# Differential attention on one core: the value unit projected within its own head and turned late, and four of ten modulation blocks computed in the last head

## The chip, the cores and the metric

The kernel runs on one core of one Trainium2 chip. The metric is the device time of one execution in microseconds (us), median of several runs. Engines: PE (TensorE) multiplies matrices, ACT (ScalarE), DVE (VectorE) and POOL (GpSimd) work elementwise, SP (SyncE) issues most of the transfers (DMA). Each engine works through its own instructions in program order and waits at semaphores, so one late operand holds up everything behind it on that engine.

## The reference

One step of a two-layer backbone: attention and a gated feed-forward layer (FFN), then an mLSTM layer and a second FFN. The change lies in the first layer's modulation and attention. `c` and `c_ctx` give the modulation of latent and context tokens:

```python
cond_p = jax.nn.silu(c_ctx)
cond_s = jax.nn.silu(c)
...
    mod_p = jnp.split(cond_p @ ada_w[i] + ada_b[i], 6, axis=-1)
    mod_s = jnp.split((cond_s @ ada_w[i] + ada_b[i])[:, None, :], 6, axis=-1)
    hp = modulate(xp, mod_p[0], mod_p[1])
    hs = modulate(xs, mod_s[0], mod_s[1])
...
        qs, ks_, vs = da_project(hs, da_w_qkv[j])
        k_all = jnp.concatenate([cache_k[:, j], rope_2d(ks_)], axis=1)
        v_all = jnp.concatenate([cache_v[:, j], vs], axis=1)
        ys = da_output(diff_attend(rope_2d(qs), k_all, v_all, lam), da_subln[j], lam_init, da_w_o[j])
...
    xs = post_norm(xs, mod_s[2] * ys, ln_g[i, 0], ln_b[i, 0])
    hs = modulate(xs, mod_s[3], mod_s[4])
```

Here the model width is 1024, there are 128 context and 512 latent tokens (640 in all), 8 heads with two 64-wide maps each and values 128 wide, and 128 cached keys and values. `diff_attend` is softmax of map 0 minus lambda times softmax of map 1, times the values. `mod[0]`, `mod[1]` are needed before the first projection; `mod[2]` first after the output projection, `mod[3]` to `mod[5]` later still.

## The kernel before

**Layout.** Activations lie with features on the partitions: 8 blocks of 128 features by 640 tokens. Everything is 32-bit; a product keeps its accuracy by splitting both operands into a high and a low part: ACT makes the high part (`whi`, `Hh`), POOL or DVE the rest (`wlo`, `Hl`), and PE multiplies high by high, low by high and high by low.

**Units.** A projection unit is 128 output columns: `q`, `k` or `v` of one head, 512 KB of weights. It is 8 tiles of 6 products each (three terms by two halves of the tokens), summed in the PSUM buffer `pj`; ACT copies it out (`evac`, L1216) before the next unit may start in the same buffer. Units run in the order q0 k0 v0 q1 k1 v1 and so on. SP loads unit n once the weights of unit n-2 are split; ACT splits (L1211), then POOL (L481).

**A head.** `head(h)` on PE mixes two things, in an order written out by hand: the attention of head h, and tiles of later units to fill PE's waits. Attention has five stages `st` (one of context tokens, four of latent ones). In a stage PE computes the scores (L811), DVE their maximum (L2039, `nmax`), ACT the exponentials (L1393), DVE the difference of the two maps (L2049 to L2054, `combine`), PE turns that by transposes into `psT` (L827, `turn`), and ACT and DVE copy it out in two parts (L1404, L2065, `turned`). `psT` is one buffer: each turn waits for `t_free` of the one before. `turn_v` (L862) turns the head's values, also in `psT`; ACT and DVE copy them out (L1443 and L1444 `values_hi`, L2095 and L2096 `values_lo`). `values_ctx` (L837) and `values_lat` (L846) multiply by the values; `values_lat` of a head runs in the next one. `rms` (L854) sums squares for the head's norm. A head takes 24 tiles of later units, except the last two: head 6 has 17, head 7 has none and takes six tiles of the output projection (`wo`).

**Rotation.** q and k are rotated (`rotate`, L2071 to L2075) with a swapped copy `sx`, which eight small transfers make (`swap`, L407, queued on SP). `sx` is one buffer: the swap of k0 waits until q0 is rotated.

**Modulation.** A block is 512 columns of `w_ada`, in 4 units of 512 KB (two feature blocks each). `block` (L660) multiplies the condition vectors by them, as rows of a PSUM tile; `copy_rows` (L1785) copies the rows to SBUF, `ada_turn` (L673) turns them, `add_bias` (L1776) adds the bias. Before, the prologue does 10 blocks: 4 ahead of everything and 6 among the projection of units 2 and 3, from an 11-deep ring of buffers `awr`. The other 14 are done in the FFN from a ring of four, `fwr`. The first latent stage of head 0 waits for `mods_ready`, which the second `add_bias` gives.

Of the kernel before, what the change touches and what calls it, by code (L numbers as in the profile page):

```python
# [157 lines left out]
def hybrid_step(nc, a, o):  # L158

    ctx = ExitStack()  # L160
    with ctx:
# [31 lines left out]
        rs = sb("rs", [P, 2, HALF])  # L193
        h32t = sb("h32t", [P, 2, TP])
        h32 = [h32t[:, k, :] for k in range(2)]
        pick = sb("pick", [P, 2 * RUN])


        with ExitStack() as s:
# [12 lines left out]
            condf = sb("condf", [P, KT, PAD + 32], F32, s)  # L212
        with ExitStack() as s:
# [4 lines left out]
            conda = sb("conda", [P, KT, PAD + 32], F32, s)  # L218
        with ExitStack() as s:
            O32 = sb("O32", [P, KT, TP], F32, s)  # L220
            v32 = sb("v32", [P, TP], F32, s)
            Qh = [sb(f"Qh{k}", [P, TP], F32R, s) for k in range(2)]
            Ql = [sb(f"Ql{k}", [P, TP], F32R, s) for k in range(2)]
            KW = TP + PAST
            Kh = [sb(f"Kh{k}", [P, KW], F32R, s) for k in range(2)]
            Kl = [sb(f"Kl{k}", [P, KW], F32R, s) for k in range(2)]
# [7 lines left out]
            rope = sb("rope", [P, 2, LAT], F32, s)  # L234
            ckv = sb("ckv", [P, 2, P], F32, s)
# [44 lines left out]
        pj = [ps(f"pj{k}", [P, 2, 512]) for k in range(1)]  # L280
        with ExitStack() as s:
# [34 lines left out]
        mods_ready = sem("mods_ready")  # L316
        mur_ready, side_ready = sem("mur_ready"), sem("side_ready")
# [45 lines left out]
        def _(sp):  # L363
# [23 lines left out]
            def load_qkv(v):  # L387
                load(a["w_qkv"][v], v // 2, v % 2, D, first=v < 2)
# [28 lines left out]
            load_ada(range(16, 27))  # L417
            sp.dma_start(rope[:, :, :], a["rope"]).then_inc(rope_in, 16)
            swap(0, 0)
            load_ada(range(27, 35))  # L420
            swap(0, 1)
            load_ada(range(35, 39))
            load_qkv(4)
            load_ada(range(39, 4 * NB))
            load_qkv(5)
            for v in range(6, U_WO + 2):
                load(a["w_qkv"][v] if v < U_WO else a["w_wo"][v - U_WO], v // 2, v % 2, D)
                if v % 3 < 2:
                    swap(v // 3 - 1, v % 3)
# [182 lines left out]
        def _(pe):  # L612
# [253 lines left out]
            def head(h):  # L866
# [10 lines left out]
                if nxt:  # L877
                    qkv(q, [7])
# [1634 lines left out]
```

## Time and profile before

| | |
|---|---|
| time, median of 3 runs | 1831.74 us (1829.88 to 1832.03) |
| the profiled execution, its own time | 1830.12 us |
| its span | 1828.3 us |
| PE busy over the span | 95% |
| DVE, ACT, POOL busy | 59%, 39%, 35% |
| prologue, up to the first scores of head 0 | 84.3 us |
| from one head's first scores to the next, heads 2 to 5 | 37.55 to 37.58 us |
| head 6; head 7 up to its `rms` | 36.07 us; 45.28 us |

Times are us from the span's start. In a timeline a row is start, length, engine, line, operation, output<-inputs, and in brackets how long the engine had been idle and what ended that. In a table of stretches a row is the stretch, its length, then busy time with the number of instructions for PE, PE's weight loads, DVE, ACT and POOL, then the granted PE clock as a share of 2.4 GHz, the busy share of the DMA engines and GB/s.

### The profile page before, as it was taken

To read this page: it belongs to the slowest core of one execution; us is meant where nothing else is said; L and a number is where in the kernel's file an instruction comes from. 1 tells how busy PE (TensorE), PEld (TensorE's weight loads), DVE (VectorE), ACT (ScalarE), POOL (GpSimd) and SP (SyncE) were. 2 spreads that over 40 slices of the span, in tenths; PEclk is the share of its full clock that TensorE was granted. 3 is DMA by queue.
4 is the path that set the end of the run, shared out by engine and by line. 5 is a ranking of instruction groups with operands and counts; after the bars stand their busy time and mean duration, and the time that the engine had idled before them with its cause. 6 is when DMAs were issued, how large, how long until landed. Compare 5 with 4: busy or idle time off the path is not lost.

```text
span 1828.3 us, 30131 instructions
## 1 busy us (share of the span) xinstructions
PE 1728.4 (95%) x11412; PEld 1608.8 (88%) x11412; DVE 1070.4 (59%) x1745; ACT 711.2 (39%) x1153; POOL 644.4 (35%) x319
## 2 busy tenths in 40 slices
PE   6899999789999999999998999998889999999996
PEld 3688888678889999999997999997879999999996
DVE  1277776657755614666457545544678781377735
ACT  3255555535432212223246544644363331132324
POOL 3312121236533333333454222222655333233343
PEclk8999999889999999999999999999999999999998
DMA  9722122111355223453211111110212222222221
GB/s 376 266 71 69 54 67 69 34 33 61 116 195 201 82 75 115 151 207 125 80 55 53 47 58 59 47 53 24 70 47 74 75 83 78 69 70 75 87 80 58
DMA packets 55191, 169.42 MB, mean 93 GB/s; under 512 B 7856, under 2 KB 15408, under 8 KB 55088
## 3 DMA queue, kind: packets, MB, share of 16 engines
q1 hardware_dynamic: 48752, 163.79, 26.1%
q10 hardware_dynamic: 6336, 4.20, 0.7%
q8 instruction: 72, 1.18, 0.3%
q14 instruction: 31, 0.25, 0.0%
HBM read 159.04 MB, written 4.72 MB: 90 GB/s over the span
## 4 chain that ended last, share of the span: by engine, by line
PE 70%; DVE 8%; POOL 7%; issue 5%; ACT 5%; DVEq 3%; DMA 2%; ACTq 1%; SPq 0%; POOLq 0%
PE pj L635 58%; POOL wlo L519 4%; DMA awr<-in_w_ada 2%; PE mO L1065 2%; PE psO L846 2%; PE psS L811 1%; PE pfrow L660 1%; POOL ss L533 1%; PE psT L827 1%; DVE pr L2054 1%; ACT pr L1393 1%; ACTq L1266 1%; POOL X L572 1%; DVE sm L2039 1%; PE mS L1021 1%
## 5 line engine op out<-in xcount | busy, mean ns | idle before, releaser
L481 POOL TENSOR_TENSOR wlo<-wraw,whi 128x1024 fp32r<-128x1024 f32 (+1 forms) x124 | 320.5, 2585 | 814.0 <-ACT whi L1211 814.0
L635 PE MATMUL pj<-Hh,whi 128*128 128x320 f32 x2368 | 568.6, 319 | 22.5 <-ACT Hh L1756 4.2
L635 PE MATMUL pj<-Hl,whi 128*128 128x320 f32 x2368 | 548.9, 311 | 3.0 <-POOL Hl L504 2.0
L635 PE MATMUL pj<-Hh,wlo 128*128 128x320 f32 x2368 | 550.7, 311 | 0.0
L635 PEld LDWEIGHTS pj<-Hh,whi 128*128 128x128 f32 x2368 | 397.8, 190 | 53.6 <-issue 37.0
L635 PEld LDWEIGHTS pj<-Hl,whi 128*128 128x128 f32 x2368 | 401.2, 190 | 4.6 <-POOL Hl L504 3.1
L635 PEld LDWEIGHTS pj<-Hh,wlo 128*128 128x128 f32 x2368 | 402.3, 190 | 0.3
L1211 ACT CAST whi<-wraw 128x1024 fp32r<-128x1024 f32 (+1 forms) x175 | 194.2, 1110 | 281.5 <-PE pj L635 241.2
L1959 DVE SCALAR_TENSOR_TENSOR fcv<-fus,vec,fcv 128x127 f32<-128x127 f32 (+1 forms) x176 | 229.1, 1343 | 15.1 <-issue 15.1
L1837 DVE SCALAR_TENSOR_TENSOR X<-pj,mods,X 128x128 f32<-128x128 f32 (+5 forms) x120 | 45.4, 434 | 219.5 <-PE pj L635 219.3
L635 PE MATMUL pj<-Gh,whi 128*128 128x320 f32 x704 | 168.8, 311 | 0.8 <-POOL wlo L519 0.8
L635 PE MATMUL pj<-Gh,wlo 128*128 128x320 f32 x704 | 167.5, 309 | 0.0
L635 PE MATMUL pj<-Gl,whi 128*128 128x320 f32 x704 | 167.5, 309 | 0.0
L1216 ACT COPY fus<-pj 128x640 f32<-128x640 f32 x88 | 60.7, 692 | 212.9 <-PE pj L635 212.7
L1962 DVE SCALAR_TENSOR_TENSOR fcv<-fus,vec,fcv 128x127 f32<-128x127 f32 (+1 forms) x176 | 120.2, 724 | 15.1 <-issue 15.1
L1956 DVE TENSOR_SCALAR fcv<-fus,vec 128x640 f32<-128x640 f32 x88 | 58.8, 668 | 107.5 <-ACT fus L1216 107.5
L635 PEld LDWEIGHTS pj<-Gh,whi 128*128 128x128 f32 x704 | 119.5, 188 | 1.6 <-POOL wlo L519 1.3
L519 POOL TENSOR_TENSOR wlo<-wraw,whi 128x1408 fp32r<-128x1408 f32 (+2 forms) x28 | 83.6, 2985 | 104.2 <-ACT whi L1211 101.9
L635 PEld LDWEIGHTS pj<-Gh,wlo 128*128 128x128 f32 x704 | 119.5, 188 | 0.3
L635 PEld LDWEIGHTS pj<-Gl,whi 128*128 128x128 f32 x704 | 119.5, 188 | 0.0
L1351 ACT CAST Gh<-fpr 128x640 f32 (+1 forms) x44 | 32.0, 728 | 214.3 <-DVE fpr L1981 214.3
L564 POOL TENSOR_TENSOR wlo<-wraw,whi 128x1024 fp32r<-128x1024 f32 x25 | 61.8, 2473 | 133.2 <-ACT whi L1211 133.2
(311 smaller groups left out, 2173.0 us busy)
## 6 DMA issues: line engine op xcount, KB each, us to landing
wraw<-in_w_up SPq DMA_DIRECT2D x88, 512.0 KB, 3.5
fwr<-in_w_ada SPq DMA_DIRECT2D x56, 512.0 KB, 5.9
wraw<-in_w_dn SPq DMA_DIRECT2D x32, 704.0 KB, 4.1
awr<-in_w_ada SPq DMA_DIRECT2D x40, 512.0 KB, 10.9
wraw<-in_w_qkv SPq DMA_DIRECT2D x24, 512.0 KB, 3.5
wraw<-in_w_mlin SPq DMA_DIRECT2D x24, 512.0 KB, 3.4
sx<-h32t SPq DMA_DIRECT2D x128, 32.0 KB, 2.0
wraw<-in_w_wo SPq DMA_DIRECT2D x8, 512.0 KB, 3.5
```

Of the source, the lines that this page charges most:

```text
L481: nc.gpsimd.tensor_tensor(wlo[k][:, 0:width], wraw[k][:, 0:width], whi[k][:, 0:width].bitcast(F32), ALU.subtract).then_inc(w_lo, 1)
L519: nc.gpsimd.tensor_tensor(wlo[k][:, c0:width], wraw[k][:, c0:width], whi[k][:, c0:width].bitcast(F32), ALU.subtract).then_inc(w_lo, 1)
L564: nc.gpsimd.tensor_tensor(wlo[v % 2][:, 0:width], wraw[v % 2][:, 0:width], whi[v % 2][:, 0:width].bitcast(F32), ALU.subtract).then_inc(w_l ...
L635: last = mm(out[:, c, 0:HALF], w, x[:, j, c * HALF:(c + 1) * HALF], start=(j == 0 and n == 0), stop=(j == n_k - 1 and n == 2))
L846: last = mm(psO[:, :], v_[par][:, c, :], t_[:, c, :], start=(c == 0 and n == 0), stop=(c == 4 and n == 2))
L1065: last = mm(mO[:, w, 0:P if part == 0 else 2 * P], v_, t_, start=(c == 0 and n == 0), stop=(c == len(terms) - 1 and n == 2))
L1211: nc.scalar.copy(whi[k][:, 0:width], wraw[k][:, 0:width]).then_inc(w_hi, 1)
L1216: nc.scalar.copy(dst.rearrange("p (a b) -> p a b", a=2), pj[k if pairs == 2 else 0][:, :, 0:HALF]).then_inc(pj_copied, 1)
L1837: last = stt(out=x, in0=pj[k][:, bank, c0:c1], scalar=gt, in1=x, op0=ALU.mult, op1=ALU.add)
L1956: ts(c[:, :], f[:, :], tap[1], bias, ALU.mult, ALU.add)
L1959: stt(out=c[:, t0 + 1:t1], in0=f[:, t0:t1 - 1], scalar=tap[0], in1=c[:, t0 + 1:t1], op0=ALU.mult, op1=ALU.add)
L1962: last = stt(out=c[:, t0:t1 - 1], in0=f[:, t0 + 1:t1], scalar=tap[2], in1=c[:, t0:t1 - 1], op0=ALU.mult, op1=ALU.add)
```

## The change

Four edits that belong together.

- **Units in another order.** `QKV_ORDER`: q0 k0 q1 k1 v0 q2 k2 v1 ... q7 k7 v6 v7. The value unit of head h is projected within head h, where v of head h+1 was.
- **Turned late.** `turn_v(h)` and `values_ctx(h)` move to the end of head h (in heads 0 to 6), on ACT and DVE too; `rms(h-1)` stands between them.
- **One unit less ahead, one more behind.** The prologue projects units 0 and 1 and seven tiles of unit 2; head 6 now has 24 tiles, and head 7 the last tile of v7.
- **Six blocks in the prologue, four in the last head.** Their 16 units are loaded into four buffers that lie over `rope`, the q and k buffers of even heads and `h32t`; they are summed in `pj` (`lrow`), so no tile of `wo` starts before `lmods_ready`. The six tiles of `wo` of head 7 follow after `scores(h, 4)`.

The unit v0 is turned with the others; `cond` is padded once, not twice. The diff, cut to its core:

```diff
+NP = 6
...
-        order += [("v", h), ("t", 5 * h), ("t", 5 * h + 1), ("t", 5 * h + 2), ("t", 5 * h + 3)]
+        if h == DA_HEADS - 1:
+            order.append(("v", h))
+        order += [("t", 5 * h), ("t", 5 * h + 1), ("t", 5 * h + 2), ("t", 5 * h + 3)]
+        if h < DA_HEADS - 1:
+            order.append(("v", h))
...
+    if what == "q":
+        return 3 * h - 1 if h else 0
+    if what == "k":
+        return 3 * h if h else 1
+    return min(3 * h + 4, 3 * DA_HEADS - 1)
...
+            def load_last():
+
+                for u in range(4 * (NB - NP)):
+                    if u == 0:
+                        sp.wait_ge(roped, 2 * DA_HEADS)
+                    elif u < 3:
+                        sp.wait_ge(sc_done, 5 * (DA_HEADS - 1))
+                    elif u == 3:
+                        sp.wait_ge(qk_ready, 2 * DA_HEADS)
+                        sp.wait_ge(kv_out[0], 16 * DA_HEADS)
+                    else:
+                        sp.wait_ge(lw_used, u - 3)
+                    sp.dma_start(lwr[u % 4][:, :, :].rearrange("p a n -> p (a n)"), a["w_ada"][4 * NP + u]).then_inc(lw_landed[u % 4], 16)
...
-            load_ada(range(16, 27))
+            load_ada(range(16, 4 * NP))
             sp.dma_start(rope[:, :, :], a["rope"]).then_inc(rope_in, 16)
             swap(0, 0)
-            load_ada(range(27, 35))
             swap(0, 1)
-            load_ada(range(35, 39))
             load_qkv(4)
-            load_ada(range(39, 4 * NB))
             load_qkv(5)
+            swap(1, 0)
...
+                scores(h, 0)
+                qkv(q, [7])
+                if prev:
+                    turn(h - 1, 4)
+                qkv(k, [0, 1])
+                if prev:
+                    values_lat(h - 1)
+                scores(h, 1)
+                qkv(k, [2, 3, 4])
+                turn(h, 0)
+                qkv(k, [5, 6])
+                scores(h, 2)
+                qkv(k, [7])
+                turn(h, 1)
+                qkv(v, [0, 1, 2, 3])
+                scores(h, 3)
+                qkv(v, [4])
+                turn(h, 2)
+                qkv(v, [5, 6, 7])
+                scores(h, 4)
+                qkv(q2, [0])
+                turn(h, 3)
+                qkv(q2, [1, 2, 3])
+                turn_v(h)
+                qkv(q2, [4, 5])
+                if prev:
+                    rms(h - 1)
+                qkv(q2, [6])
+                values_ctx(h)
+
+            def last_head(h):
...
                 scores(h, 0)
+                qkv(3 * DA_HEADS - 1, [7])
+                turn(h - 1, 4)
+                last_blocks([0, 1])
+                values_lat(h - 1)
                 scores(h, 1)
                 turn_v(h)
+                last_blocks([2, 3])
                 turn(h, 0)
+                last_blocks([4])
                 scores(h, 2)
+                last_blocks([5])
                 turn(h, 1)
                 values_ctx(h)
+                last_blocks([6, 7])
                 scores(h, 3)
                 turn(h, 2)
+                last_turn()
                 scores(h, 4)
+                pe.wait_ge(lmods_ready, 1)
+                wo([0])
                 turn(h, 3)
+                wo([1, 2, 3])
+                rms(h - 1)
+                wo([4, 5]).then_inc(part_used, 1)
...
             first_pair(0, h_ready, 0, 0)
             ada_block(4)
+            qkv(2, [0, 1])
             ada_block(5)
-            qkv(2, [0, 1, 2, 3])
-            ada_block(6)
...
-            qkv(3, [6])
+            qkv(2, [2, 3, 4, 5, 6])
             ada_turn(1)
...
+            def last_head(h):
+                combine(h - 1, 4)
+                nmax(h, 0)
...
+                combine(h, 2)
+                nmax(h, 3)
+                copy_last()
+                turned(h, 2)
+                combine(h, 3)
+                nmax(h, 4)
+                dve.wait_ge(lrow_turned, 1)
+                add_bias(lmod, 4 * NP, NB - NP)
+                turned(h, 3)
```

**SP's queue at the end of the prologue.** SP before, from the last loads ahead of `rope`; `awr` are modulation units, `sx` the swaps of q0 and then k0.

```order
L377 DMA awr<-in_w_ada 128x1024 x11
L418 DMA rope<-in_rope 128x1024
L407 DMA sx<-h32t 16x512 x8
L377 DMA awr<-in_w_ada 128x1024 x8
L407 DMA sx<-h32t 16x512 x8
L377 DMA awr<-in_w_ada 128x1024 x4
L371 DMA wraw<-in_w_qkv 128x1024
L377 DMA awr<-in_w_ada 128x1024
L371 DMA wraw<-in_w_qkv 128x1024 x2
L407 DMA sx<-h32t 16x512 x8
```

SP in the changed kernel, from the same place.

```order
L404 DMA awr<-in_w_ada 128x1024 x8
L459 DMA rope<-in_rope 128x1024
L448 DMA sx<-h32t 16x512 x16
L398 DMA wraw<-in_w_qkv 128x1024 x2
L448 DMA sx<-h32t 16x512 x8
L398 DMA wraw<-in_w_qkv 128x1024
L448 DMA sx<-h32t 16x512 x8
```

The two swaps now stand next to each other (x16): 13 modulation loads between and behind them are gone, and three of the eleven ahead of `rope`.

**PE's queue at the end of head 2.** PE before, from `rms` to the next head's first scores.

```order
L635 MATMUL pj<-Hl,whi 128x320 x2
L854 MATMUL psT<-ss,ones 128x320 x2
L635 MATMUL pj<-Hh,whi 128x320 x2
L635 MATMUL pj<-Hh,wlo 128x320 x2
L635 MATMUL pj<-Hl,whi 128x320 x2
L635 MATMUL pj<-Hh,whi 128x320 x2
L635 MATMUL pj<-Hh,wlo 128x320 x2
L635 MATMUL pj<-Hl,whi 128x320 x2
L635 MATMUL pj<-Hh,whi 128x320 x2
L635 MATMUL pj<-Hh,wlo 128x320 x2
L635 MATMUL pj<-Hl,whi 128x320 x2
L811 MATMUL psS<-Kh,Qh 128x128
```

PE in the changed kernel, from `turn_v` (L919) over `rms` (L911) to the first product of `values_ctx` (L894), behind whose three products the next head's scores stand.

```order
L919 MATMUL psT<-ident,v 128x128 x5
L680 MATMUL pj<-Hh,whi 128x320 x2
L680 MATMUL pj<-Hh,wlo 128x320 x2
L680 MATMUL pj<-Hl,whi 128x320 x2
L680 MATMUL pj<-Hh,whi 128x320 x2
L680 MATMUL pj<-Hh,wlo 128x320 x2
L680 MATMUL pj<-Hl,whi 128x320 x2
L911 MATMUL psT<-ss,ones 128x320 x2
L680 MATMUL pj<-Hh,whi 128x320 x2
L680 MATMUL pj<-Hh,wlo 128x320 x2
L680 MATMUL pj<-Hl,whi 128x320 x2
L894 MATMUL psO<-Aph,Vh 128x128
```

`turn_v` and `values_ctx` now stand here; they stood behind the scores and behind the turn of stage 1. `rms` has one tile and `values_ctx` behind it where it had three tiles.

**PE's queue in the middle of head 7.** PE before: the turn of stage 1, `values_ctx`, two tiles of `wo`, the scores of stage 3.

```order
L827 MATMUL psT<-ident,pr 128x128 x5
L837 MATMUL psO<-Aph,Vh 128x128
L837 MATMUL psO<-Apl,Vh 128x128
L837 MATMUL psO<-Aph,Vl 128x128
L635 MATMUL pj<-Hh,whi 128x320 x2
L635 MATMUL pj<-Hh,wlo 128x320 x2
L635 MATMUL pj<-Hl,whi 128x320 x2
L635 MATMUL pj<-Hh,whi 128x320 x2
L635 MATMUL pj<-Hh,wlo 128x320 x2
L635 MATMUL pj<-Hl,whi 128x320 x2
L811 MATMUL psS<-Kh,Qh 128x128
```

PE in the changed kernel: between `values_ctx` and the scores stand the four units of the fourth block.

```order
L705 MATMUL pj<-lwk,condp 32x512 x2
L705 MATMUL pj<-lwh,condp 32x512 x2
L884 MATMUL psT<-ident,pr 128x128 x5
L894 MATMUL psO<-Aph,Vh 128x128
L894 MATMUL psO<-Apl,Vh 128x128
L894 MATMUL psO<-Aph,Vl 128x128
L705 MATMUL pj<-rope,condp 32x512 x2
L705 MATMUL pj<-lwq,condp 32x512 x2
L705 MATMUL pj<-lwk,condp 32x512 x2
L705 MATMUL pj<-lwh,condp 32x512 x2
L868 MATMUL psS<-Kh,Qh 128x128
```

The scores of stage 3 now stand behind products that wait for transfers.

## Rows read from the trace of the kernel before

**Rows 1.** Busy time by stretch: end of prologue, head 4, head 6, head 7.

```profile
52.00:84.20 32.20, 28.30 (x195) 16.99 (x194) 7.11 (x11) 6.63 (x10) 7.08 (x3) 1.00 0.75 275
230.24:267.80 37.56, 36.36 (x247) 32.54 (x247) 27.29 (x49) 20.50 (x42) 7.21 (x3) 1.00 0.22 64
305.35:341.42 36.07, 31.36 (x205) 26.80 (x204) 25.82 (x48) 19.05 (x40) 6.09 (x3) 0.95 0.23 67
341.42:386.70 45.28, 35.27 (x189) 28.96 (x189) 25.58 (x43) 21.68 (x44) 12.74 (x8) 0.81 0.04 12
```

**Rows 2.** Chain that ended last, in the prologue: start, us, what.

```profile
63.37 3.73 PE pj L635 x24
...
70.98 10.35 DMA awr<-in_w_ada
...
84.28 0.49 PE psS L811 x6
```

**Rows 3.** Timeline of SP in the prologue, the two swaps.

```profile
52.49 5.01 SPq L407 DMA_DIRECT2D sx<-h32t  x8
...
62.56 4.93 SPq L407 DMA_DIRECT2D sx<-h32t  x8
```

**Rows 4.** Timeline of DVE in the prologue: rotations, k0's low part, rows copied.

```profile
59.00 0.98 DVE L2071 TENSOR_TENSOR sx<-sx,rope 128x512 f32<-128x512 f32 x1 [8.53 <-DMA sx<-h32t]
...
60.66 0.69 DVE L2075 TENSOR_TENSOR h32t<-h32t,sx 128x512 f32<-128x512 f32 x1
...
74.27 0.69 DVE L2071 TENSOR_TENSOR sx<-sx,rope 128x512 f32<-128x512 f32 x1 [11.30 <-DMA sx<-h32t]
...
77.13 0.83 DVE L2088 TENSOR_TENSOR Kl<-h32t,Kh 128x640 fp32r<-128x640 f32 x1 [0.21 <-ACT Kh L1438]
82.47 0.69 DVE L1785 COPY arow<-prow 128x512 f32<-128x512 f32 x1 [4.51 <-PE prow L660]
```

**Rows 5.** Timeline of PE in head 4: `turn_v`, two turns, first of `values_ctx`.

```profile
239.51 0.76 PE L862 MATMUL psT<-ident,v 128*128 128x128 f32 x5
...
247.59 0.77 PE L827 MATMUL psT<-ident,pr 128*128 128x128 f32 x5 [0.37 <-DVE pr L2054]
248.11 0.31 PE L837 MATMUL psO<-Aph,Vh 128*128 128x128 f32 x1
...
260.72 0.77 PE L827 MATMUL psT<-ident,pr 128*128 128x128 f32 x5 [0.45 <-DVE pr L2054]
```

**Rows 6.** Timeline of ACT in head 4: values copied out, high part.

```profile
240.31 0.58 ACT L1443 CAST Vh<-psT 128x512 fp32r<-128x512 f32 x1 [1.47 <-PE psT L862]
```

**Rows 7.** Timeline of DVE in head 4: last low values; `combine` at head's end.

```profile
241.86 0.28 DVE L2096 TENSOR_TENSOR Vl<-psT,Vh 128x128 fp32r<-128x128 f32 x1
...
265.06 2.39 DVE L2051 TENSOR_TENSOR sm<-sm,lam 128x1 f32<-128x1 f32 x1
```

**Rows 8.** Timeline of POOL in head 4, the third unit's low part.

```profile
265.01 2.42 POOL L481 TENSOR_TENSOR wlo<-wraw,whi 128x1024 fp32r<-128x1024 f32 x1 [9.94 <-ACT whi L1211]
```

**Rows 9.** Busy time by stretch in heads 6 and 7, where the clock was low.

```profile
339.00:351.60 12.60, 9.30 (x26) 6.51 (x27) 7.65 (x15) 5.13 (x12) 5.51 (x3) 0.50 0.13 42
368.70:375.30 6.60, 5.34 (x25) 4.51 (x25) 4.63 (x9) 2.66 (x6) 0.43 (x1) 0.50 0.00 0
```

**Rows 10.** Timeline of PE in head 7: scores of stages 2 and 3, last turn.

```profile
358.96 0.33 PE L811 MATMUL psS<-Kh,Qh 64*128 64x128 f32 x1
...
364.57 0.32 PE L811 MATMUL psS<-Kh,Qh 64*128 64x128 f32 x1 [0.57 <-ACT pr L1393]
...
379.04 0.77 PE L827 MATMUL psT<-ident,pr 128*128 128x128 f32 x5 [0.28 <-DVE pr L2054]
```

**Rows 11.** Timeline of DVE in head 7: `combine` of stage 2, last step.

```profile
365.49 2.23 DVE L2054 SCALAR_TENSOR_TENSOR pr<-pr,sm 128x640 f32<-128x640 f32 x1
```

**Rows 12.** Timeline of PE in the FFN: one modulation block.

```profile
496.24 1.92 PE L660 MATMUL pfrow<-fwr,condf 128*32 128x512 f32 x16
```

**Rows 13.** All instructions on the tile `fwr`: issue to landing, units of 512 KB.

```profile
DMA to landing us min/median/max: 3.5/5.9/7.8
```

More of the change, by code:

```diff
@@ L111, with _qkv_unit @@
 QT = (4, 0, 1, 2, 3)
+def _qkv_unit(what, h):
+    if what == "q":
[3 more added lines that the diff above has]
+    return min(3 * h + 4, 3 * DA_HEADS - 1)
+QKV_ORDER = [at for _, at in sorted((_qkv_unit(what, h), 3 * h + c) for h in range(DA_HEADS) for c, what in enumerate("qkv"))]
 GROWS = 100
@@ L316, in hybrid_step @@
         mods_ready = sem("mods_ready")
+        lw_landed = [sem(f"lw_landed{k}") for k in range(4)]
+        lw_used, lrow_copied, lrow_turned, lmods_ready = (
+            sem(n) for n in ("lw_used", "lrow_copied", "lrow_turned", "lmods_ready"))
         mur_ready, side_ready = sem("mur_ready"), sem("side_ready")
@@ L651, in first_pair, with block @@
                         tile(pair, k, [j], pairs=2, terms=(2,))
-            def block(b, n, out, conds, bufs, landed, used, at):
-                for kp in range(4):
+            def block(b, n, out, conds, bufs, landed, used, at, kps=range(4)):
+                for kp in kps:
                     u = at + kp
@@ L866, in head @@
             def head(h):
-                nxt, nxt2, prev, last = h + 1 < DA_HEADS, h + 2 < DA_HEADS, h > 0, h + 1 == DA_HEADS
-                q, k, v, q2 = (3 * h + 3 + c for c in range(4))
+                prev = h > 0
+                q, k, v, q2 = (3 * h + 2 + c for c in range(4))
+                scores(h, 0)
[28 more added lines that the diff above has]
+            def last_head(h):
                 def wo(ks):
@@ L1466, in head @@
             def head(h):
-                nxt, prev, last = h + 1 < DA_HEADS, h > 0, h + 1 == DA_HEADS
-                k, v, q2, k2 = (3 * h + 4 + c for c in range(4))
-                if nxt:
-                    copy_q(h + 1)
+                prev = h > 0
+                copy_q(h + 1)
                 if prev:
@@ L1778, in add_bias @@
                     last.then_inc(mods_ready, 1)
+                if t0 == 4 * NP:
+                    last.then_inc(lmods_ready, 1)
                 dve.drain()
             def copy_rows(k):
-                dve.wait_ge(aw_used, 4 * NB if k else 16)
+                dve.wait_ge(aw_used, 4 * NP if k else 16)
                 if k:
@@ L2140, in _ @@
             dve.wait_ge(row_turned, 2)
-            add_bias(pmod[1], 2 * KT, 6)
-            for h in range(DA_HEADS):
+            add_bias(pmod[1], 2 * KT, NP - 4)
+            for h in range(DA_HEADS - 1):
                 head(h)
+            last_head(DA_HEADS - 1)
             combine(DA_HEADS - 1, 4)
```

205 lines of the change are left out of this document (99 added, 106 removed).

## The prediction

> **What bounds the kernel now.** I read four stretches, each by its table of busy time, then its timelines, and the chain for the prologue. In the end of the prologue the DMA engines are busy for 0.75 of the time and PE gets through 28.3 us of short work in 32.2 [rows 1]; the chain there runs through a modulation load that takes 10.35 us to come, and reaches head 0's first scores at 84.28 [rows 2]. A middle head is PE's: 36.36 us busy of 37.56 [rows 1]. What is left are three short waits, two of them for DVE's difference of the maps, 0.37 and 0.45 us [rows 5]. Head 6 has 17 tiles and is hardly shorter, 36.07 us. Head 7 is 45.28 us with a mean clock of 0.81 [rows 1]: there the serial chain of a stage (scores, maximum, exponentials) sets the pace, 5.6 us from one stage's scores to the next [rows 10], and the clock is at half for 12.6 and 6.6 us [rows 9]. So the change has a load-bound stretch to shorten, seven full stretches in which every added PE instruction counts, and one with room in it whose order matters.
>
> The sum is made on the profiled execution, 1830.12 us with a span of 1828.3; it is 1.6 us under the median of the three runs, 1831.74.
>
> **1. Prologue: -11.0.** Head 0's scores need k0 rotated. Its swap is issued at 62.56 [rows 3] and lands only at 74.27, for which DVE waited 11.30 us [rows 4]: eight modulation loads were queued ahead of it. Without them the swap may be issued when q0 is rotated, 60.66 + 0.69 = 61.35 [rows 4]. q0's own swap was issued at 52.49 [rows 3] and DVE started at 59.00 [rows 4], 6.5 us later; so k0 starts at 67.85. From there to k0's low part is 77.13 + 0.83 - 74.27 = 3.7 us, and from the copy of the rows to the scores 84.28 - 82.47 = 1.8 us [rows 2, 4], since that copy stands behind k0 on DVE: 73.35. Before it was 84.28. PE is through by about 65: two blocks and seven tiles (0.93 each, 3.73 for four [rows 2]) from 52. The four removed blocks cost nothing else here. Bounds: -12 if the swap also issues faster, -9 if the two loads of units 4 and 5 get in its way.
>
> **2. Clock at the restart: +1.5.** PE is now idle for some 8 us before head 0. In head 6 the clock fell to 0.50 after waits of 2 to 3 us and stayed there 12.6 us, and later 6.6 [rows 9]. Low for 3 to 6 us of mostly PE-bound work costs half of that, less the waits in it: 1.5, between 0 and 3. The gap itself is in no row before; if the clock stayed up, the sum would be 1.5 less.
>
> **3. The late turn: +6.0.** Per head, from the order on PE:
> - `turn_v` leaves the place behind the scores of stage 1. Its five transposes last 0.76 [rows 5] with their drain, under which the next product starts; I take 0.5. That gives nothing: the turn of stage 1 waits for DVE [rows 5], and DVE's chain starts at those scores (maximum, exponentials, rotation of q, difference), none of which gets shorter. The wait grows from 0.37 to 0.9 us.
> - `values_ctx` leaves, about 0.4 (three products, the first [rows 5]): -0.4, and all behind it moves up, the next wait for DVE too, as its chain starts at the scores of stage 3.
> - At the end `turn_v` comes back, +0.6 with the change of operand type, and `values_ctx`, +0.4.
> - `rms` needs `psT`, which `values_lo` now frees. ACT starts 0.8 us after `turn_v` (239.51 to 240.31 [rows 5, 6]); its two copies take 0.75 (0.58 the first [rows 6]), DVE's two subtractions 0.9 (0.28 the last [rows 7]), with the hand-overs 2.6 us. PE covers 0.5 + 2 x 0.93 = 2.35 of it: +0.25.
>
> Together 0.6 + 0.25 = 0.86 us a head; seven heads, less the first, which has no `rms`: 6.0. At a head's end DVE also runs into POOL: an operation on 128x1 took 2.39 us, from 265.06, beside POOL's 2.42 from 265.01 [rows 7, 8]. It does so in both kernels; `combine` of the last stage then comes 0.9 later, just as the head does. Bounds: 0.5 (no wait at `rms`) and 1.3 a head (0.4 more where ACT is late with the values), so 3.5 to 9. The other moved edits of ACT and DVE sit in their idle time (20.5 and 27.3 us busy of 37.56 [rows 1]) and cost nothing; if `values_hi` met the exponentials it would cost their 1.6 us, which is in the upper bound.
>
> **4. Head 6 gets its seven tiles back: +1.5.** It lasted 36.07, full ones 37.56 [rows 1].
>
> **5. Head 7: +5.2.** It begins at full clock now. Times from its first scores, work at full clock:
> - A last tile of v7 (0.9), its copy, the block of four units that landed in head 6 (1.9 [rows 12]), then `values_lat`: scores of stage 1 at 7.9 (before 11.4, at half clock).
> - The ring is four buffers. A unit's buffer is free when PE has used it, and the next one lands 3.5 us after issue alone, up to 7.8 as the fourth of four [rows 13], so 1.3 to 1.4 apart. Units 4 to 7 are used at 10.3 to 11.7; unit 9, issued at 10.8, lands at 15.2. Scores of stage 2 stand behind it: 15.75. The chain alone would have let them go at 14.1.
> - Unit 15 is issued at 18.2 and lands at 22.4; the scores of stage 3 stand behind it: 23.0 (before 23.15 [rows 10], so still even). Then one free chain: scores of stage 4 at 27.85.
> - `wo` must wait for `lmods_ready`. On DVE that stands behind `combine` of stage 3 and the maximum of stage 4. `combine` will meet POOL's low part of `wo`'s input, as it did once before in this head, 2.23 us for one step instead of 0.9 [rows 11]. It ends at 31.1, the maximum at 33.0, the bias at 33.3. PE idles for 4 us.
> - Then six tiles of `wo` (5.4), a turn, `rms`, one tile more: last turn at 41.1. Before it was at 379.04 - 341.42 = 37.6 [rows 1, 10]. So +3.5, and what follows is the same.
> - The idle 4 us bring the clock down again: +1.7 (low 3 to 5 us, half lost [rows 9]).
>
> The Trainium skill (SBUF — State Buffer, Who interferes with whom) says that of a DVE operation with two SBUF inputs and a GpSimd operation that reads SBUF the later one is blocked until the other is through, and that copies and scalar operations between SBUF tiles can be caught too. By it the small operation behind the maximum of stage 4 could be caught as well, for as long as the step in [rows 11] was, 1.3 us more.
>
> Bounds for head 7: +1 (units land 3.5 us apart from issue each, no POOL collision, no low clock) and +10 (all transfers like the slowest in [rows 13], and the clock low through the second half).
>
> **Sum.** -11.0 + 1.5 + 6.0 + 1.5 + 5.2 = +3.2: 1833.3 us for an execution like the profiled one, 1834.9 on the median. I give 1834.5. The padding of the condition vectors that goes from the FFN (one copy and one memset on DVE) was under DVE's slack: nothing, at most -0.7.
>
> **Rivals.**
> - **A. Faster, about 1824.** `turn_v` late costs nothing, because PE's waits for DVE shrink as much as the end of the head grows, and head 7's blocks fall into its waits (10 us idle of 45.28 [rows 1]): -11.0 + 1.5 + 1.5 + 0 to 1 = -7.5. For it: PE waits three times in a head. Against it: the waits hang on a chain that starts at PE's own scores. It decides where the head period stays at 37.6.
> - **B. Slower, about 1840.** Head 7's tail: everything that waited for `pj` comes after the scores of stage 4. If the bias is ready only after the whole stage (ACT's exponentials of stage 4 ahead of DVE), and the clock stays at half through the six tiles of `wo` (5.4 us more), the head costs 10 to 11 instead of 5.2: +8 to +9. It decides if the idle time before `wo` is over 5 us. For it: the half clock after shorter gaps [rows 9]. Against it: the chain of DVE as written ends at 33.3.
> - **C. The prologue does not shorten as said**, since something else than the loads holds k0 (the copy of v0, which also leaves, or unit 3's split): gain 5 instead of 11, +9, about 1840. Against it: the 11.30 us wait names the swap's DMA [rows 4].
>
> **How the numbers follow.** Chances: forecast 0.52, A 0.15, B 0.28, C 0.05. A change of 0.2% is 3.7 us, about what a measurement of this kernel can tell from none. The forecast's own range, 1827 to 1837, crosses that limit on both sides: of its 0.52 some 0.07 is slower and 0.03 faster. So faster 0.15 + 0.03 = 0.18, same 0.42, slower 0.28 + 0.05 + 0.07 = 0.40. The range, 1826 to 1842, leaves out most of A and the far ends of B and C.
>
> **What the changed profile would show.** Step 1: first scores of head 0 at 73 to 75, DVE's wait for the swap under 7 us. Step 2: half clock at the start of head 0. Step 3: heads 38.2 to 38.7 us apart, a short wait of `rms` for the low values. Step 4: head 6 as long as the others. Step 5: head 7 some 48 to 52 us, with waits of the last blocks of modulation for `w_ada` and one of 4 us before the first tile of `wo`. What would make me wrong: a head period under 38, or a tail of head 7 in which `wo` is not held.

## The result, and the profile after

The changed kernel takes 1839.18 us (median of five runs, 1837.65 to 1841.11), the kernel before 1829.95 beside it (five runs): ratio 1.0050, 95% interval 1.0039 to 1.0062. It is slower by 0.5%, some 9 us. The profiled executions differ by 7.5 us (1837.65 against 1830.12). The value forecast was 1834.5 and the range 1826 to 1842; slower had a chance of 0.40, no measurable change 0.42.

I read four stretches of the changed kernel. Busy time by stretch: end of the prologue, head 4, head 6, head 7 up to its `rms`, and the part of head 7 at half clock (columns as in [rows 1]):

```profile
62.00:73.20 11.20, 6.13 (x38) 5.86 (x36) 4.09 (x8) 0.72 (x1) 0.00 (x0) 0.87 0.36 115
225.06:263.28 38.22, 36.54 (x247) 32.58 (x247) 27.29 (x49) 20.38 (x43) 7.23 (x3) 1.00 0.21 63
301.55:339.78 38.23, 36.53 (x247) 32.57 (x247) 27.28 (x49) 20.39 (x43) 7.22 (x3) 1.00 0.38 118
339.78:394.23 54.45, 46.36 (x268) 32.10 (x267) 25.82 (x44) 22.50 (x46) 14.51 (x8) 0.91 0.38 137
371.00:381.30 10.30, 8.38 (x39) 7.81 (x39) 5.61 (x9) 3.33 (x8) 3.62 (x2) 0.52 0.00 0
```

Beside [rows 1]: head 4 is 0.66 us longer for 0.18 us more PE work, head 6 is now a full head, and head 7, up to its `rms`, has grown from 45.28 to 54.45.

The prologue, on DVE (k0's swap, its low part, the copy of the rows) and then on PE:

```profile
67.08 0.69 DVE L2144 TENSOR_TENSOR sx<-sx,rope 128x512 f32<-128x512 f32 x1 [4.90 <-DMA sx<-h32t]
...
69.93 0.83 DVE L2161 TENSOR_TENSOR Kl<-h32t,Kh 128x640 fp32r<-128x640 f32 x1 [0.20 <-ACT Kh L1498]
70.67 0.68 DVE L1855 COPY arow<-prow 128x512 f32<-128x512 f32 x1
```

```profile
71.41 1.87 PE L732 MATMUL pmod<-pick,arow 128*128 128x4 f32 x8 [5.07 <-DVE arow L1855]
73.20 0.48 PE L868 MATMUL psS<-Kh,Qh 64*128 64x128 f32 x2
```

The swap's wait fell from 11.30 [rows 4] to 4.90 us and the first scores came at 73.20 for 84.22. But PE stood idle for 5.07 us first, and then the turn of the rows took 1.87 us, at half clock.

A middle head, on PE (turn of stage 1, turn of the values, `rms`, first of `values_ctx`):

```profile
242.29 0.77 PE L884 MATMUL psT<-ident,pr 128*128 128x128 f32 x5 [0.76 <-DVE pr L2127]
...
258.32 0.71 PE L919 MATMUL psT<-ident,v 128*128 128x128 f32 x5
260.88 1.31 PE L911 MATMUL psT<-ss,ones 128*128 128x320 f32 x4
262.90 0.22 PE L894 MATMUL psO<-Aph,Vh 128*128 128x128 f32 x1
```

The turn of stage 1 waits 0.76 us where it waited 0.37 [rows 5]: taking the values' turn away from before it only lengthened the wait.

Head 7, the chain of work that ended last (start, us, what). The two transfers in it are loads of `w_ada`; the last four lines are `wo`'s first tile and what it waited for (DVE's maximum of stage 4, the small operation behind it, and the drain behind the bias):

```profile
351.39 4.76 DMA lwq<-in_w_ada
...
357.25 1.36 PE psS L868 x10
...
360.00 5.78 DMA lwh<-in_w_ada
...
366.88 1.37 PE psS L868 x10
...
370.65 1.87 PE pj L724 x8
372.53 2.40 PE psS L868 x10
...
374.96 1.49 DVE sm L2112
...
376.52 0.17 DVE sm L2114
...
376.69 0.10 DVEq L1849
...
376.84 1.97 PE pj L680 x6
```

The scores of stages 2 and 3 stand behind loads. PE's waits in this head, two for loads of `w_ada` and the two in the tail, ahead of the turn of the row and of `wo`:

```profile
354.94 1.05 PE L705 MATMUL pj<-rope,condp 128*32 128x512 f32 x4 [1.94 <-DMA rope<-in_w_ada]
...
364.56 1.05 PE L705 MATMUL pj<-lwk,condp 128*32 128x512 f32 x4 [1.42 <-DMA lwk<-in_w_ada]
...
370.65 1.87 PE L724 MATMUL pj<-pick,v 128*128 128x8 f32 x8 [1.72 <-DVE v L1860]
...
376.84 0.90 PE L680 MATMUL pj<-Hh,whi 128*128 128x320 f32 x2 [1.92 <-DVE mods L1844]
```

From the turn of the row (L724) to about 381 all of PE's work is at half clock (1.2 of 2.4 GHz): the scores of stage 4 take 2.40 us for 1.37.

Where the 7.5 us lie, in us, from the first scores of each head in the two traces: first scores -11.0; head 0 +3.2; head 1 +1.3; heads 2 to 5 +2.8; head 6 +2.2; head 7 up to its `values_lat` +9.1 (49.16 for 40.03).

### The profile page after: what moved, and what is told of

It is laid out like the page before. It is cut to its first block, busy times and chain, and to the rows that moved or that the text cites. A ratio compares the mean times of both kernels' runs of the same rounds, so it can differ in the third digit from the quotient of the medians.

```text
span 1835.9 us, 30150 instructions
## 1 busy us (share of the span) xinstructions
PE 1732.7 (94%) x11420; PEld 1613.8 (88%) x11420; DVE 1070.0 (58%) x1745; ACT 710.6 (39%) x1153; POOL 644.5 (35%) x319
## 4 chain that ended last, share of the span: by engine, by line
PE 71%; DVE 8%; POOL 6%; issue 5%; ACT 4%; DVEq 2%; DMA 2%; ACTq 1%; SPq 1%; POOLq 0%
PE pj L680 59%; POOL wlo L564 4%; PE mO L1124 2%; PE psS L868 2%; PE psO L903 2%; PE pfrow L705 1%; DMA awr<-in_w_ada 1%; POOL ss L578 1%; PE psT L884 1%; ACTq L1325 1%; DVE pr L2127 1%; DVE sm L2112 1%; PE mS L1080 1%; DVE h32t L2148 1%; ACT pr L1452 1%
```

## The experiments

Each is compared with the kernel before on the same chip. The runs fall into three sets on three chips (e1 to e4, e5 to e8, e9 to e12), in which the kernel before had medians of 1829.96, 1829.50 and 1830.00 us. Times are medians; the lengths are from one profiled execution each, so a difference of lengths and one of medians need not agree. Heads 0 and 4 are counted from their first scores to those of the next head, head 7 from its first scores to its `values_lat`.

| run | us | ratio to before (95%) | first scores | head 0 | head 4 | head 7 |
|---|---|---|---|---|---|---|
| before | 1829.50 to 1830.00 | | 84.22 | 33.02 | 37.56 | 40.03 |
| changed | 1839.18 | 1.0050 (1.0039 to 1.0062) | 73.20 | 36.18 | 38.22 | 49.16 |
| e1, turn only | 1836.53 | 1.0037 (1.0024 to 1.0049) | 83.59 | 35.95 | 38.21 | 36.78 |
| e2, blocks only | 1832.43 | 1.0021 (1.0011 to 1.0032) | 74.98 | 33.56 | 37.58 | 51.67 |
| e3, four loads | 1832.39 | 1.0012 (1.0003 to 1.0021) | 72.98 | 36.27 | 38.27 | 43.08 |
| e4, filler | 1836.32 | 1.0030 (1.0017 to 1.0043) | 73.06 | 34.91 | 38.25 | 49.34 |
| e5, early hand-over | 1832.91 | 1.0019 (1.0009 to 1.0028) | 73.84 | 36.04 | 38.22 | 42.67 |
| e6, e2 with ring of 8 | 1829.06 | 0.9996 (0.9987 to 1.0005) | 76.04 | 34.54 | 37.58 | 46.13 |
| e7, e6 and e5's edit | 1822.40 | 0.9966 (0.9955 to 0.9976) | 75.85 | 34.56 | 37.56 | 41.55 |
| e8, changed with ring of 8 | 1831.93 | 1.0017 (1.0008 to 1.0026) | 73.50 | 36.06 | 38.25 | 42.82 |
| e9, e7, a block in head 6 | 1826.05 | 0.9980 (0.9972 to 0.9989) | 74.76 | 33.37 | 37.55 | 43.59 |
| e10, e8 and e5's edit | 1826.99 | 0.9984 (0.9975 to 0.9993) | 72.19 | 35.96 | 38.26 | 38.77 |
| e11, before, turn twice | 1833.54 | 1.0023 (1.0015 to 1.0032) | 84.10 | 33.56 | 38.09 | 40.35 |
| e12, changed, turn twice | 1845.90 | 1.0089 (1.0075 to 1.0104) | 71.83 | 36.50 | 38.79 | 51.31 |

**The two halves of the change: e1 and e2.** e1 is the changed kernel with all blocks in the prologue (their loads placed as before) and none in head 7:

```
-NP = 6
+NP = 10
...
             turn(h, 0)
-            last_blocks([4])
+            wo([0, 1])
             scores(h, 2)
...
-            last_turn()
+            wo([4])
             scores(h, 4)
-            pe.wait_ge(lmods_ready, 1)
```

> The changed kernel with all ten modulation blocks back in the prologue (loads and products interleaved as before), no block and no turn of them in head 7, and wo's six tiles back in their old places there. What is left of the change is the unit order with the late turn of the values. Theory T (the head period read from the changed trace): 38.25 us for 37.55 in heads 0 to 5 (+4.2), head 6 full for 36.07 (+2.2), one more tile in head 7 (+0.9), nothing in the prologue: +7.3 us, 1837. Rival R (the order of the units costs little, and nearly all of the loss is the blocks in head 7): +1 to +3, 1831 to 1833.

e2 is the other half, the blocks moved with the units in their old order (an edit of the changed kernel):

```
-    return min(3 * h + 4, 3 * DA_HEADS - 1)
+    return 3 * h + "qkv".index(what)
...
                 scores(h, 1)
+                turn_v(h)
...
                 turn(h, 1)
+                values_ctx(h)
...
-                turn_v(h)
...
-                values_ctx(h)
```

> The other half: unit order, early turn of the values and weights' queue as before, but blocks 6 to 9 in head 7 with their loads, turn and bias as in the changed kernel. Theory T: prologue -11.0, head 0 +3.7 (clock at half and the wait for the first copy), head 7 +8 (9.2 less the tile of the value unit): +0.7 us, 1830.7, between 1828 and 1833. If the turn and the blocks are independent, this and the run of the turn alone add up to the changed kernel (+9.2 by the medians). Rival R (the blocks are the loss): 1836 to 1838.

The turn and order alone cost 6.6 us, the blocks alone 2.5; together 9.0, the change 9.2 (by the ratios 0.37% and 0.21% for 0.50%). Both totals are what theory T said, and the rival (most of the loss is the blocks) falls. The parts behind the totals are not what T said, so that they agree is in part luck:

- e1: head 0 grew by 2.9 us, where T had 0.7, and head 7 became 3.3 us shorter, where T had 0.9 more. Before, head 7 runs at a mean clock of 0.79; in e1, whose head 6 has tiles to its end, at 0.91.
- e2: the first scores came 9.2 us earlier (T: 11.0), head 0 grew by 0.5 (T: 3.7), head 7 by 11.6 (T: 8). The blocks alone thus pay 11.6 us in head 7 for 9.2 in the prologue.

In e1's trace head 4 is as long as in the changed kernel, and its head 0 is long too, though its first scores are as late as before; I had put that down to the shorter prologue. Head 0 of e1, of e2, and the first tile of its second unit in e1 and in e2:

```profile
83.59:119.54 35.95, 33.81 (x224) 30.82 (x223) 23.38 (x45) 16.89 (x36) 5.86 (x3) 0.91 0.18 52
```

```profile
74.98:108.54 33.56, 31.26 (x224) 28.45 (x223) 23.99 (x45) 17.16 (x37) 6.44 (x3) 1.00 0.22 65
```

```profile
86.91 0.87 PE L682 MATMUL pj<-Hh,whi 128*128 128x320 f32 x2 [0.93 <-ACT h32t L1278]
```

```profile
77.54 0.53 PE L669 MATMUL pj<-Hh,whi 128*128 128x320 f32 x2 [0.93 <-ACT h32t L1275]
```

The wait of 0.93 us is the same in both kernels (and before), but the clock is at half in e1, from 84.2 on, and at full in e2. What differs ahead of the fall, between e1 and the kernel before, are the eight tiles of unit v0, which the kernel before and e2 have in the prologue and the late order has not. In e2 PE's tiles go on up to 74.1, just ahead of the first scores; in e1 PE stands idle six times between 70 and 83, 4.35 us in all, for loads and for the copy of the rows. The late turn, which e1 has too, is not what brings the clock down, since it stands behind the fall; but no run puts the eight tiles back alone. Nor are they the whole story: e6, e7 and e9 have e2's prologue and head 0, and in e6 and e7 the clock fell in head 0 too, for 3.4 us, and it took 34.5 to 34.6 us. With the tiles head 0 took 33.0 to 34.6 us, without them and without the filler of e4 36.0 to 36.3 (six kernels).

**The clock at the restart: e4.** 32 products in PE's gap, whose results nothing reads:

```
             qkv(2, [2, 3, 4, 5, 6])
+            for _ in range(32):
+                mm(psS[:, 0:HALF], whi[0][:, 0:P], Hh[:, 0, 0:HALF], start=True, stop=True)
             ada_turn(1)
```

> The changed kernel with 32 products of 128x320 put into the 5.07 us in which PE waits for the copy of the rows in the prologue; they write the scores' bank, which head 0's scores overwrite, so no result hangs on them. Theory T (the fall of the clock to 0.50 is what head 0 lost: turn of the rows 1.87 us at half clock, tiles at 0.73 for 0.46 a pair up to 80.9): 3 to 4 us less, 1835.5. Rival (head 0's chain is what counts and the low clock hides behind it, or the clock falls nevertheless): 0 to -1, 1838 to 1839.

1836.32 us, 2.9 less by the medians; in the profiled execution head 0 is 1.27 us shorter. The median is near theory T, the trace between the two: the clock stayed up through the turn and the first tile, and then was at half behind the wait of 0.93 us nevertheless. Busy time of e4 in steps of 2 us:

```profile
74.00:76.00 2.00, 1.07 (x7) 0.84 (x6) 0.27 (x2) 1.22 (x5) 0.00 (x0) 0.96 0.01 4
76.00:78.00 2.00, 2.00 (x10) 2.00 (x9) 0.87 (x4) 1.12 (x3) 0.81 (x1) 0.50 0.17 38
```

The changed kernel, e3, e5, e8 and e10 have one prologue and one head 0, and head 0 took 35.96 to 36.27 us in them; e4's 34.91 lies 1.0 to 1.4 us below all five. So much of the 3.2 us in head 0 is shown to be the low clock; the filler doesn't remove all of it, and how much the rest of it costs was not measured.

**The loads of head 7: e3, e8, e6.** e3 issues only four of the sixteen, so it leaves out the weights of blocks 7 to 9:

```
-                for u in range(4 * (NB - NP)):
+                for u in range(4):
```

> The changed kernel with only the first four of the sixteen loads of w_ada in head 7: blocks 7, 8 and 9 take the weights of block 6, so the modulation they give is that of block 6's weights. All products, the turn, the bias and the order stay. Theory T (the ring of four buffers delays the scores of stages 1 to 3: waits of 1.94, 1.42 and some 0.8 us in head 7, and they bring the clock down): head 7 shorter by 4 to 7 us, 1832 to 1835. Rival (the serial chain of a stage sets the pace, and a wait for a load only takes the place of one for the chain): -1 or less, 1838 to 1839.

Head 7 is 43.08 for 49.16, the time 6.8 us less: theory T, but for one part of it. That the waits for loads bring the clock down is not borne out: without them head 7 has a mean clock of 0.88, with them 0.90. The cause could still be the depth of the ring or the bandwidth. e8 and e6 keep all loads and lay four more buffers over tiles 4 to 7 of `Hh` and `Hl`, which nothing reads after the last value tile:

```
-            lwr = [rope, lwq, lwk, lwh]
+            lwr = [rope, lwq, lwk, lwh, lwx[0][1], lwx[1][1], lwx[0][0], lwx[1][0]]
...
-                        sp.wait_ge(lw_used, u - 3)
+                        sp.wait_ge(lw_used, u - 7)
```

> The changed kernel itself with the ring of eight; here the four new buffers are free only when the last value tile is done early in head 7, so they stand behind the four old ones in the ring. Theory T: units 4 to 7 are issued some 8 us earlier than now, the waits of 1.94, 1.42 and 0.8 us go: -3 to -5 us, 1835. Rival (bandwidth): -1 or less, 1838.5.

> The kernel with only the blocks moved (before's unit order), its ring of w_ada units made eight deep: four more buffers lie in the tiles 4 to 7 of Hh and Hl, free once the last value unit's product is done in head 6, and they come first in the ring, so half of the sixteen units are under way before head 7. Same work and order otherwise. Theory T (head 7 waits for loads because only four can be under way; run with four loads: 6 us): 4 to 6 us less than the kernel with only the blocks moved, 1826.5 to 1828.5. Rival (DMA bandwidth, not the depth, is the bound): -1 or less, 1831.5.

Head 7 of e8:

```profile
339.90:382.72 42.82, 37.05 (x240) 25.29 (x240) 26.75 (x44) 21.17 (x44) 13.02 (x8) 0.92 0.46 174
```

That is no longer than with twelve loads left out, and the time is 7.3 us less than the changed kernel's, more than T's 3 to 5 (6.0 by the ratios). Depth was the bound, bandwidth was not. e8's waits for loads in head 7 are down to two of 0.23 us. In e6, with before's order, head 7 is 5.5 us shorter than in e2, as T said, but the medians differ by only 3.4 (4.6 by the ratios); in e6's profiled execution head 0 was 1.0 us longer than e2's, though nothing was changed there.

**The hand-over and the held `wo`: e5.** The row is copied earlier and turned into `psO`; in place of `wo`, `values_lat` at the end of the head waits for `lmods_ready`, and the bias stands on DVE ahead of `combine` of stage 3. The edit, cut:

```
-        lmod = pj[0][:, 1, 0:32].rearrange("p (q w) -> p q w", q=4)
+            lmod = psO[:, 0:32].rearrange("p (q w) -> p q w", q=4)
...
+                if h == DA_HEADS - 1:
+                    pe.wait_ge(lmods_ready, 1)
...
                 last_turn()
+                wo([0, 1])
                 scores(h, 4)
-                pe.wait_ge(lmods_ready, 1)
-                wo([0])
+                wo([2])
                 turn(h, 3)
-                wo([1, 2, 3])
+                wo([3])
...
                 combine(h, 2)
+                copy_last()
                 nmax(h, 3)
-                copy_last()
                 turned(h, 2)
+                dve.wait_ge(lrow_turned, 1)
+                add_bias(lmod, 4 * NP, NB - NP)
                 combine(h, 3)
...
```

> The changed kernel with the hand-over of head 7's blocks made earlier and wo not held by it: DVE copies the row ahead of the maximum of stage 3 instead of behind it, the turn of the row goes to the bank of psO, which is free then, so wo's tiles in pj wait only for the copy; two tiles of wo before the scores of stage 4, one before the turn of stage 3, one behind it, two behind rms. Same work. Theory T (the tail of head 7 pays for being held: waits of 1.72 and 1.92 us, and with them the clock at half for 10 us): last turn 46.8 to about 42 us behind the head's start, -4 to -5 us, 1834.5. Rival (the chain of stages 3 and 4 sets the end, the held wo only fills it): -0 to -1.5, 1838.

Head 7 with the edit:

```profile
340.19:382.86 42.67, 37.40 (x240) 23.79 (x239) 25.78 (x44) 21.29 (x44) 13.09 (x8) 1.00 0.49 175
```

Head 7 is 6.5 us shorter in the profiled execution, and the medians differ by 6.3, more than T's 4 to 5. The clock fits that: 1.00 for the whole of head 7, where it was 0.90. The two waits (1.72 and 1.92 us) were 3.6 us; with them went the stretch at half clock. How the 6.5 us divide between the two was not measured. The turn of the row had to leave `pj` altogether, since a tile of `wo` writes both halves of `pj`. The Trainium skill (PSUM — Partial Sum Buffer, Summary: rules for kernel authors) says that PSUM read while a matmul runs should be in a different bank than the one written, and `psO` is one. No run here shows what a shared bank would do.

**Both repairs, in before's order and in the late one: e7, e10.**

> Blocks moved, before's unit order, ring of eight, and the early hand-over with wo not held. Theory T (load waits and held wo are two separate costs): about 1823, 7 us under before. Rival (only one of them is on the path at a time): as the better of the two, 1827.

> The changed kernel with both repairs of head 7 (ring of eight, early hand-over of the row with wo not held) and its late turn of the values kept. Theory T (late turn and unit order cost 6.6 us by themselves, whatever head 7 does): 1822.4 + 6.5, so 1828 to 1829, no better than before. Rival (the early turn's gain overlaps with the repairs): 1824 to 1825.

e7 takes 1822.40 us, 0.34% under the kernel before, about what T said; it is the fastest version. In before's order the ring gave 3.4 us and the hand-over 6.7 on top of it (medians). Whether the two costs are separate is seen in the changed kernel's order, where all four versions were run: head 7 is 49.16 us as it was, 42.82 with the ring (e8), 42.67 with the hand-over (e5), 38.77 with both (e10). The gains are 6.3, 6.5 and 10.4: separate for the most part, and 2.4 us are counted in both.

e10 is 4.6 us slower than e7 by the medians (0.18% by the ratios), less than the 6.5 expected and more than the rival's 2 to 3. The profiled executions don't show that difference: they are 0.3 us apart, 1826.86 for e10, which is near its median, and 1826.52 for e7, which is the second longest of its eleven (1820.24 to 1827.18). In them e10 is 7.6 us longer from first scores to head 7 (266.4 for 258.8), which is the late turn, the full head 6 and the clock of head 0; its first scores are 3.7 earlier and its head 7 is 2.8 shorter. It has full clock in head 7, where e7 has half up to 341 and again from 362 to 365. The granted clock over the whole of e7's execution was 0.978 in the profiled one and 0.981 to 0.983 in the six shortest, which suggests that these had less half clock; no trace shows where. Head 7 of e7 and of e10:

```profile
334.64:376.19 41.55, 37.00 (x234) 24.92 (x233) 27.86 (x45) 20.36 (x42) 11.73 (x8) 0.88 0.44 164
```

```profile
338.58:377.35 38.77, 35.86 (x241) 23.71 (x240) 26.52 (x44) 21.27 (x44) 13.10 (x8) 1.00 0.50 192
```

**What a turn of the values costs in each place: e11, e12.** Five transposes done twice, in the kernel before and in the changed one:

```
-                for c in range(5):
+                for c in (0, 1, 2, 3, 4, 0, 1, 2, 3, 4):
```

> The kernel before with the five transposes of the values done twice in their early place, the second five over the first: 0.46 us more PE work a head. Theory T of the late turn (behind the scores of stage 1 the turn lies under the wait for DVE's difference of the maps, 0.37 us, and on the path only with the rest): the wait goes to nothing and the head period grows by about 0.1 us, 37.55 to 37.65, in all +1 us, not more than the measurement can tell. Rival (PE's work counts wherever it stands): +0.46 a head, 38.0, in all +3.5 us.

> The changed kernel with the same doubling in the late place. Theory T: nothing there waits for DVE's maps, so all of it is paid, +0.45 us a head, 38.25 to 38.7, +3 us in all. Rival (the wait of rms for the values' low part takes it up, or the head's start absorbs it): +0.1 a head or less, 0 to +1 us.

Head 4 of the kernel before so changed, and its turn of stage 1:

```profile
232.28:270.37 38.09, 36.88 (x252) 33.07 (x252) 27.40 (x49) 20.41 (x42) 7.18 (x3) 1.00 0.22 63
```

```profile
250.16 0.76 PE L827 MATMUL psT<-ident,pr 128*128 128x128 f32 x5 [0.37 <-DVE pr L2054]
```

e11 refutes theory T for the early place: +0.53 us a head, all of it paid, and the wait is still 0.37. e12 pays 0.57, as T said (its 6.7 us by the medians are more than seven heads of that; head 7 is 2.1 us longer too). The wait of 0.37 us is no slack. It hangs on the turn of stage 0: ACT copies that out (`Aph`), DVE takes the low part, rotates q and then makes the difference that the wait is for. The turn of stage 0 stands behind `turn_v` on PE and moves with it. In the kernel before it comes just as ACT is through with the exponentials of stage 1, and ACT takes `Aph` up at once; in e11 it comes later, and ACT waits 0.43 us for it; in the changed kernel it comes sooner, and ACT is still at the exponentials. ACT's exponentials' last step and the copy, before and in the changed kernel, and the copy in e11 (the turn of stage 0 starts at 242.75, 237.07 and 245.33):

```profile
242.85 0.20 ACT L1393 ACTIVATION_READ_ACCUMULATOR pr<-psS,sm 128x1 f32 x1
243.06 0.27 ACT L1401 CAST Aph<-psT 128x128 fp32r<-128x128 f32 x1
```

```profile
237.67 0.20 ACT L1452 ACTIVATION_READ_ACCUMULATOR pr<-psS,sm 128x1 f32 x1
237.76 0.26 ACT L1460 CAST Aph<-psT 128x128 fp32r<-128x128 f32 x1
```

```profile
245.64 0.27 ACT L1401 CAST Aph<-psT 128x128 fp32r<-128x128 f32 x1 [0.43 <-PE psT L827]
```

From the scores of stage 1 to this copy it is 4.91 us before, 4.79 in the changed kernel and 5.45 in e11. So two chains were level there, one through PE's own work and one through the exponentials: less PE work gains 0.1 us, more costs in full.

**A block at the end of head 6: e9.**

```
+                if not nxt2:
+                    last_blocks([0])
                 if prev:
                     rms(h - 1)
+                if not nxt2:
+                    last_blocks([1])
```

> The fastest kernel so far (blocks moved, before's unit order, ring of eight, early hand-over; 1822.4) with the first of the four blocks done at the end of head 6, before and behind rms of head 5, where PE has no tiles, and the other pieces one place earlier in head 7. Same work. Theory T (head 6's end waits 1.5 and 2.4 us for DVE and the clock is at half afterwards): the block is hidden there and head 7 starts at full clock, -2 to -4 us, 1819 to 1820. Rival (the loads of the first four units are not in by then, so PE waits for them at head 6's end and delays rms and the last scores): 0 to +1, 1823.

Neither theory: by the medians 3.6 us slower than e7 (0.14% by the ratios, whose intervals overlap a little), in the profiled executions 1.4. It is not for the loads, for which PE waited once, 0.34 us. The clock stays up in head 6 (0.99 from 328 to 336), but it is at half for 3.4 us at the start of head 7 all the same, and head 7 has a block less to put under its stages: 43.59 us for e7's 41.55. Its waits come back at stage 3, and the half clock with them (0.53 from 356 to 367):

```profile
355.19 0.32 PE L870 MATMUL psS<-Kh,Qh 64*128 64x128 f32 x1 [2.02 <-ACT pr L1471]
358.40 1.33 PE L886 MATMUL psT<-ident,pr 128*128 128x128 f32 x5 [1.62 <-DVE pr L2160]
```

How much of the loss is the clock and how much the stages' chain was not separated.

## Why the prediction held in range and missed in size

The forecast was 1834.5 us and the range held the 1839.18. The sum was +3.2 us on the profiled execution; it was +7.5. Of the 4.3 us that were missing 3.9 lie in head 7. Point by point:

- **Step 1, prologue, -11.0: right** in its reason, and in its size with a little luck. First scores came 11.0 us earlier, the swap's wait was 4.90 us ("under 7"). k0's rotation started at 67.08, 0.8 us ahead of the forecast 67.85, and from the copy of the rows to the scores it took 2.5 us for a forecast 1.8, because the turn of the rows ran at half clock. The two misses cancel.
- **Step 2, clock at the restart, +1.5: too small**, within its bounds of 0 to 3. Head 0 grew by 3.2 us, of which some 0.6 is the late turn; 2.6 is left. And the reason was incomplete: I tied the low clock to the gap that the missing blocks leave. e1 has the blocks in the prologue and loses 2.9 us in head 0; e2 lacks them there and loses 0.5, or 1.5 in e6 and e7. The two long head 0s have in common that the eight tiles of v0 are gone from the prologue, which I had counted as a removal that costs nothing. The waits ahead of the half clock in head 6, which the step calls 2 to 3 us, were 1.53 and 2.43 in the trace.
- **Step 3, late turn, +6.0: right in size**, for heads 0 to 6. Its own terms give 0.86 x 7 - 0.25 = 5.8. It came to 0.66 to 0.72 a head in heads 2 to 5 for a forecast 0.86, and to 5.4 or so in all; head 1 has 0.57 more, in every kernel with the late order, and its cause was not looked for. The wait of stage 1's turn went to 0.76 (forecast 0.9), and `rms` starts 0.25 us later behind its tile than before. That the early turn had been hidden was right as a balance, wrong as a slack (e11).
- **Step 4, head 6, +1.5: right**: 2.2 less the late turn's 0.7.
- **Step 5, head 7, +5.2: the step that failed**, +9.1. Its mechanism was right (scores behind loads, `wo` held, a half clock), two of its terms were too small. Against the times forecast from the head's start: scores of stage 1 at 8.1 (7.9), stage 2 at 17.4 (15.75), stage 3 at 27.0 (23.0), stage 4 at 32.7 (27.85), first tile of `wo` 37.1 (33.3), last turn 46.8 (41.1). So it was 4.0 us late at the scores of stage 3 and 5.7 at the last turn.
  - The loads. Units 9 and 15 were to take 4.4 and 4.2 us from issue to landing and took 4.76 and 5.78. They were issued 0.8 and 2.0 us later than said, unit 15 because PE frees units 10 and 11 only behind the scores of stage 2, which an earlier load had held. A ring of eight takes 6.3 us off head 7 (e8).
  - The tail. The waits were 1.72 and 1.92 us, shorter than the one of 4 that I forecast, but with a half clock of 10.3 us, where I allowed for 3 to 5 us of it at a cost of 1.7. The early hand-over takes 6.5 us off (e5).

  Both repairs together take 10.4 of the 12.4 us that separate head 7 from e1's.
- **DVE beside POOL**: forecast once more at stage 3, and it came. The last step of `combine` took 2.07 us, for 0.89 where POOL is idle, beside POOL's low part of `wo`'s input:

```profile
372.67 2.07 DVE L2127 SCALAR_TENSOR_TENSOR pr<-pr,sm 128x640 f32<-128x640 f32 x1
```

```profile
372.52 3.62 POOL L549 TENSOR_TENSOR Hl<-O,Hh  x2 [5.12 <-ACT Hh L1510]
```

By the rule of the Trainium skill (SBUF — State Buffer, Who interferes with whom) the small operation behind the maximum of stage 4 could have been caught as well, for 1.3 us. Here it took 0.17 us, and POOL was idle by then, since 376.14. The trace of the kernel before bears the rule out for this operation, in stage 2 of its head 7: it took 0.83 us for 0.17 elsewhere, and ended with POOL's work at 362.8.

```profile
361.99 0.83 DVE L2041 TENSOR_SCALAR sm<-sm 128x2 f32<-128x2 f32 x1
```

```profile
359.46 3.33 POOL L504 TENSOR_TENSOR Hl<-O,Hh  x2 [8.74 <-ACT Hh L1450]
```

- **Rivals.** A fell: the head period went to 38.2. B named the place and nearly the price (head 7 at 10 to 11 instead of 5.2, 1840), but its condition, over 5 us idle ahead of `wo`, was not met: PE waited 1.92 us there. Its half clock came. So B is nearer in number than in reason. C fell: the swap landed as forecast.

## What to carry to other kernels

Work that is moved into a latency-bound stretch costs little if its data are there and nothing is held for it: against e1, the same four blocks cost head 7 12.4 us with a ring of four and `wo` held, and 2.0 with a ring of eight and an early hand-over. Count what a removed piece of work was covering: the eight tiles taken out of the prologue were "free", and without them head 0 took 36.0 to 36.3 us for 33.0 to 34.6. A short wait is slack only if its chain does not begin behind the work that is to fill it; follow it back to the first instruction on the waiting engine.

## What was not expected of the hardware

- The length of one wait does not tell whether the clock falls. In the changed kernel's head 7 it stayed at 1.00 behind a wait of 1.94 us for a load, and behind one of 1.72 us in the tail it was at half for 10 us. In e5 it stayed at 1.00 through one of 1.74 us for a load and ones of 0.17, 0.57 and 0.84 us in the tail; in e4 it was at half behind one of 0.93 us, and in e1 and the changed kernel the same wait came when it was at half already.
- The same instructions do not always get the same clock. e2, e6, e7 and e9 have one prologue and one head 0; head 0 took 33.56, 34.54, 34.56 and 33.37 us, with mean clocks of 1.00, 0.95, 0.95 and 1.00. So a difference of 1 us in that stretch of one trace says nothing by itself. e4's gain counts because the five kernels that it is measured against lie within 0.3 us.
